# First weights in pieces beside the inputs, part of the banded attention's elementwise work on GpSimd, and one row maximum over two PSUM banks

## What is computed

```python
for l in range(2):                                   # kind A
    proj = rms_norm(x, norm_mix_w[l]) @ w_in[l]
    mixed = concat(blocked_gqa(q, k, v), ssd_mixer(...))
    x = x + mixed @ w_out[l]
    h = rms_norm(x, norm_ffn_w[l])
    x = x + (silu(h @ w_gate[l]) * (h @ w_up[l])) @ w_down[l]
x = rms_norm(x, final_norm_w)                        # "residual scaling"
for l in range(2):                                   # kind B
    proj = rmsnorm(x, g_attn[l]) @ w_in_2[l]
    ya = windowed_gqa_sink(qa, ka, va, sink[l])      # keys within 128 tokens
    yb = diff_attention(qb, kb, vb, lam)             # softmax 1 - lam * softmax 2
    x = x + concat(ya, norm(yb)) @ w_out_2[l]
    x = x + (silu(conv3(h @ gate)) * (h @ val)) @ w_down_2[l]
```

## Time and profile before

| | |
|---|---|
| time of the kernel before | 2509.87 us median of 3 runs (2509.07 to 2510.38) |
| profiled execution: time, and span from first to last instruction | 2512.78 us, 2510.6 us |
| busy share: PE, DVE, ACT, POOL | 97%, 59%, 38%, 8% |
| granted TensorE clock, mean | 0.991 of full speed |
| first matmul starts | 13.55 us |
| banded attentions, window of each | layer 2: 1366 to 1434 us; layer 3: 1993 to 2062 us |

### The profile page before, as it was taken

The page is one execution under the profiler, slowest core; times in us unless marked ns, Lnnn a source line. Parts: engine busy times, 40 slices in busy tenths (PEclk is TensorE's granted clock), DMA queues, the critical chain, the costliest instruction groups (busy, mean ns, idle before and its releaser), DMA issues.

```text
span 2510.6 us, 30919 instructions
## 1 busy us (share of the span) xinstructions
PE 2430.3 (97%) x12468; PEld 1989.0 (79%) x12468; DVE 1474.9 (59%) x2074; ACT 944.8 (38%) x1496; POOL 210.5 (8%) x143
## 2 busy tenths in 40 slices
PE   7999999999999999999999799999999989999999
PEld 6767888888876788888887578888888767888887
DVE  5867543435586754343567766545466776655554
ACT  4465322213446432222444563222243465322222
POOL 2001200000200110000132011000012101100000
PEclk9999999999999999999999899999999999999999
DMA  4200222222311032222321002222232110222222
GB/s 172 78 35 1 101 96 89 101 101 101 102 68 35 1 103 99 101 95 90 118 84 68 35 9 102 94 100 101 91 111 99 53 35 25 94 101 101 100 85 101
DMA packets 30238, 205.32 MB, mean 82 GB/s; under 512 B 3344, under 2 KB 3472, under 8 KB 6288
## 3 DMA queue, kind: packets, MB, share of 16 engines
q1 hardware_dynamic: 30096, 203.35, 22.8%
HBM read 201.24 MB, written 2.10 MB: 81 GB/s over the span
## 4 chain that ended last, share of the span: by engine, by line
PE 85%; DVE 8%; DVEq 3%; ACT 2%; issue 1%; ACTq 0%; DMA 0%; POOL 0%; SPq 0%
PE bank L1568 25%; PE bank L1570 25%; PE bank L1569 25%; PE bank L1727 1%; PE bank L1671 1%; PE bank L1703 1%; PE bank L1953 1%; PE bank L1901 1%; PE bank L1714 1%; PE bank L1654 1%; DVE w_lo L771 1%; DVE b_p L1435 1%; DVE neg_max L1423 1%; ACT w_hi L321 1%; DVEq L1430 1%
## 5 line engine op out<-in xcount | busy, mean ns | idle before, releaser
L771 DVE TENSOR_TENSOR w_lo<-w_raw,w_hi 128x2048 fp32r<-128x2048 f32 (+1 forms) x190 | 434.0, 2284 | 404.9 <-ACT w_hi L321 404.4
L1568 PE MATMUL bank<-h_ffn_hi,w_hi 128*128 128x512 f32 x1408 | 548.6, 390 | 0.0
L1570 PE MATMUL bank<-h_ffn_hi,w_lo 128*128 128x512 f32 x1408 | 547.8, 389 | 0.0
L1569 PE MATMUL bank<-h_ffn_lo,w_hi 128*128 128x512 f32 x1408 | 547.7, 389 | 0.0
L321 ACT ACTIVATE w_hi<-w_raw 128x2048 fp32r<-128x2048 f32 (+1 forms) x190 | 360.1, 1895 | 473.0 <-PE bank L1570 424.5
L1570 PEld LDWEIGHTS bank<-h_ffn_hi,w_lo 128*128 128x128 f32 x1408 | 264.3, 188 | 55.1
L1569 PEld LDWEIGHTS bank<-h_ffn_lo,w_hi 128*128 128x128 f32 x1408 | 264.3, 188 | 54.7
L1568 PEld LDWEIGHTS bank<-h_ffn_hi,w_hi 128*128 128x128 f32 x1408 | 264.3, 188 | 54.5
L1568 PE MATMUL bank<-act_hi,w_hi 128*128 128x512 f32 x704 | 273.9, 389 | 0.0
L1569 PE MATMUL bank<-act_lo,w_hi 128*128 128x512 f32 x704 | 273.9, 389 | 0.0
L1570 PE MATMUL bank<-act_hi,w_lo 128*128 128x512 f32 x704 | 273.9, 389 | 0.0
(11 more groups left out here) (305 smaller groups left out, 3396.3 us busy)
## 6 DMA issues: line engine op xcount, KB each, us to landing
w_raw<-weights SPq DMA_DIRECT2D x186, 1024.0 KB, 4.7
w_raw<-weights SPq DMA_DIRECT2D x4, 544.0 KB, 3.7
residual<-x_in SPq DMA_DIRECT2D x8, 256.0 KB, 5.8
x_out<-residual SPq DMA_DIRECT2D x8, 256.0 KB, 2.0
cst<-consts SPq DMA_DIRECT2D x1, 960.0 KB, 10.2
par_b<-params_b SPq DMA_DIRECT2D x1, 627.0 KB, 11.2
par_a<-params_a SPq DMA_DIRECT2D x1, 244.0 KB, 2.7
```

The costliest lines, as they stand in the source:

```text
L771: nc.vector.tensor_tensor(w_lo[s][:, cols], w_raw[s][:, cols], w_hi[s][:, cols].bitcast(F32), ALU.subtract).then_inc(w_ready, 1)
L1568: mm(out, ahi, bhi, start=start, stop=False)
L1569: mm(out, ahi, blo, start=False, stop=False)
L1570: return mm(out, alo, bhi, start=False, stop=stop)
```

## The change

- **Start.** Weights 0 and 1 come as 8 quarters of 128 x 512, each ahead of one tile of x. ACT, DVE split a quarter and then a tile of x, with the square of a tile one tile later. `first_pair` on PE goes over the 8 feature tiles, each with all four token tiles, and has `stats(0)` ahead of the last feature tile.
- **Opening of kind B.** ACT splits group `g0 + 2` before it waits for `rstd`.
- **Banded attention.** ACT splits groups `g0 + 9` and `g0 + 10` in halves, in steps 4, 5 and 8, 9. GpSimd makes their remainders, one instruction of 128 x 2048 each. In layer 2 GpSimd also scales `residual`, with two instructions of 128 x 4096, one behind each remainder. DVE waits for both before the additions of the output projection.
- **Row maxima.** In all three attentions one DVE instruction reduces both banks of a step. The 8 banks become one tensor for it.

```diff
@@ -181,11 +181,18 @@
...
         gate, silu, up = ([Fb[f"{n}{j}"] for j in range(2)] for n in ("gate", "silu", "up"))
-        bank = [ctx.enter_context(nc.psum_tensor(f"bank{j}", [P, 512], F32)) for j in range(8)]
+        banks = ctx.enter_context(nc.psum_tensor("bank", [P, 8, 512], F32))
+        bank = [banks[:, j, :] for j in range(8)]
+
+        def both_banks(pair, width):
+
+            return banks[:, pair[0]:pair[1] + 1, 0:width]
         par_in = sem("par_in")
+        first_in = [sem(f"first_in{k}") for k in range(KT)]
+        first_hi, first_ready = sem("first_hi"), sem("first_ready")
         x_arrived = [sem(f"x_arrived{k}") for k in range(KT)]
...
@@ -293,10 +304,10 @@
             sp.dma_start(par_a[:, :, :], params_a).then_inc(par_in, 16)
-            sp.dma_start(w_raw[0][:, :], weights[0]).then_inc(w_in[0], 16)
             for k in range(KT):
+                cols = first_cols(k)
+                sp.dma_start(w_raw[k // 4][:, cols], weights[k // 4][:, cols]).then_inc(first_in[k], 16)
                 sp.dma_start(residual[:, k, :], x_in[:, k, :]).then_inc(x_arrived[k], 16)
-            sp.dma_start(w_raw[1][:, :], weights[1]).then_inc(w_in[1], 16)
             sp.dma_start(cst[:, :], consts).then_inc(consts_in, 16)
...
@@ -314,11 +325,20 @@
...
                 s = g % 2
-                act.wait_ge(w_in[s], 16 * (g // 2 + 1))
-                if g >= 2:
-                    act.wait_ge(bank_done, 2 * (g - 2) + 2)
+                act.wait_ge(w_in[s], 16 * (g // 2))
+                act.wait_ge(bank_done, 2 * (g - 2) + 2)
                 cols = slice(0, width_of(g))
                 nc.scalar.activation(w_hi[s][:, cols], w_raw[s][:, cols], ACT.Copy).then_inc(w_hi_done, 1)
+
+            def split_half(g, part):
+
+                s = g % 2
+                act.wait_ge(w_in[s], 16 * (g // 2))
+                act.wait_ge(bank_done, 2 * (g - 2) + 2)
+                cols = slice(part * GW // 2, (part + 1) * GW // 2)
+                nc.scalar.activation(w_hi[s][:, cols], w_raw[s][:, cols], ACT.Copy)
+                if part == 1:
+                    act.drain().then_inc(w_hi_done, 1)
             def wait_tile(lay, tile):
@@ -467,12 +487,15 @@
...
             act.wait_ge(par_in, 16)
-            split_hi(0)
             for k in range(KT):
+                cols = first_cols(k)
+                act.wait_ge(first_in[k], 16)
+                nc.scalar.activation(w_hi[k // 4][:, cols], w_raw[k // 4][:, cols], ACT.Copy).then_inc(w_hi_done if k % 4 == 3 else first_hi, 1)
                 wait_tile(-1, 24 + k)
                 norm_hi(h_mix_hi, k, mix_weight(0, k))
-                norm_square(0, k)
-            split_hi(1)
+                if k >= 1:
+                    norm_square(0, k - 1)
+            norm_square(0, KT - 1)
             for lay in range(LAYERS):
...
@@ -675,8 +698,8 @@
...
                 nc.scalar.activation(lam[:, 2:4], lam[:, 0:2], ACT.Exp).then_inc(lam_out, 1)
+                split_hi(g0 + 2)
                 act.wait_ge(rstd_ready, 2 * lay + 1)
-                split_hi(g0 + 2)
                 for half in range(2):
...
@@ -706,8 +729,8 @@
...
                         sink_exp(i // 4 - 1)
-                    if i in (12, 14):
-                        split_hi(g0 + 3 + i // 2)
+                    if i in (4, 5, 8, 9):
+                        split_half(g0 + IN_B + i // 8, i % 2)
                     if i - 1 in TURN_STEPS:
...
@@ -891,11 +914,9 @@
             def pair_max(lay, i):
-                for par_ in range(2):
-                    c = 2 * i + par_
-                    dve.wait_ge(s_done, 32 * lay + c + 1)
-                    nc.vector.tensor_reduce(neg_max[:, c:c + 1], bank[S_BANKS[i % 2][par_]][:, :], AX.X, ALU.max,
-                                            negate=True).then_inc(max_done, 1)
+                dve.wait_ge(s_done, 32 * lay + 2 * i + 2)
+                nc.vector.tensor_reduce(neg_max[:, 2 * i:2 * i + 2], both_banks(S_BANKS[i % 2], 512), AX.X, ALU.max,
+                                        negate=True).then_inc(max_done, 2)
             def pair_copy(lay, u, width, pts):
@@ -968,10 +989,15 @@
...
             dve.wait_ge(par_in, 16)
-            split_lo(0)
             for k in range(KT):
+                s, cols = k // 4, first_cols(k)
+                if k % 4 == 3:
+                    dve.wait_ge(w_hi_done, s + 1)
+                else:
+                    dve.wait_ge(first_hi, 3 * s + k % 4 + 1)
+                nc.vector.tensor_tensor(w_lo[s][:, cols], w_raw[s][:, cols], w_hi[s][:, cols].bitcast(F32),
+                                        ALU.subtract).then_inc(w_ready if k % 4 == 3 else first_ready, 1)
                 norm_lo(0, h_mix_hi, h_mix_lo, k, mix_weight(0, k))
-            split_lo(1)
             dve.wait_ge(consts_in, 16)
...
@@ -1367,11 +1393,9 @@
                 def window_max(i):
-                    for par_ in range(2):
-                        c = 2 * i + par_
-                        dve.wait_ge(s_done, base + c + 1)
-                        nc.vector.tensor_reduce(neg_max[:, c:c + 1], bank[S_BANKS[i % 2][par_]][:, 0:window(i // 4)[1] * P],
-                                                AX.X, ALU.max, negate=True)
+                    dve.wait_ge(s_done, base + 2 * i + 2)
+                    nc.vector.tensor_reduce(neg_max[:, 2 * i:2 * i + 2], both_banks(S_BANKS[i % 2], window(i // 4)[1] * P),
+                                            AX.X, ALU.max, negate=True)
                     dve.drain()
...
@@ -1404,12 +1428,6 @@
...
                         pair_copy(lay, i - 2, window((i - 2) // 4)[1] * P, pts)
-                    if i in (12, 14):
-                        split_lo(g0 + 3 + i // 2)
-                    if l == 0 and 7 <= i < 7 + KT:
-                        k = i - 7
-                        nc.vector.scalar_tensor_tensor(residual[:, k, :], residual[:, k, :], par_a[:, 0, A_FIN + k:A_FIN + k + 1],
-                                                       rstd_bc[:, :], ALU.mult, ALU.mult)
                     if i >= 6 and i % 4 == 2:
...
@@ -1476,6 +1492,9 @@
...
                     nc.vector.memset(gate[j][:, SEQ + 1:SEQ + 2], 0.0)
+                if l == 0:
+                    dve.wait_ge(x_scaled, 1)
+                dve.wait_ge(w_ready, g0 + IN_B + 2)
                 for g in range(QUARTERS):
...
@@ -1548,6 +1567,25 @@
...
                                                 ALU.pow).then_inc(hrs_ready, 1)
+
+                def split_lo(g):
+
+                    s = g % 2
+                    pool.wait_ge(w_ready, g)
+                    pool.wait_ge(w_hi_done, g + 1)
+                    nc.gpsimd.tensor_tensor(w_lo[s][:, :], w_raw[s][:, :], w_hi[s][:, :].bitcast(F32), ALU.subtract).then_inc(w_ready, 1)
+
+                g0 = FIRST[lay]
+                split_lo(g0 + IN_B)
+                if l == 0:
+                    pool.wait_ge(bc_ready, broadcasts(2 * lay) + 1)
+                    x = residual[:, :, :]
+                    nc.gpsimd.tensor_tensor(x, x, par_a[:, 0, A_FIN:A_FIN + KT].unsqueeze(2).to_broadcast([P, KT, SEQ]), ALU.mult)
+                    pool.drain()
+                    split_lo(g0 + IN_B + 1)
+                    nc.gpsimd.tensor_tensor(x, x, rstd_bc[:, :].unsqueeze(1).to_broadcast([P, KT, SEQ]), ALU.mult).then_inc(x_scaled, 1)
+                else:
+                    split_lo(g0 + IN_B + 1)
                 def diff_factors(t):
...
@@ -1605,6 +1643,25 @@
...
                 last.then_inc(bank_done, 1)
+
+            def first_pair():
+
+                for k in range(KT):
+                    s, kk = divmod(k, 4)
+                    if kk == 3:
+                        pe.wait_ge(w_ready, s + 1)
+                    else:
+                        pe.wait_ge(first_ready, 3 * s + kk + 1)
+                    pe.wait_ge(h_ready, k + 1)
+                    if k == KT - 1:
+                        pe.wait_ge(consts_ready, 1)
+                        stats(0)
+                    for t in range(TB):
+                        ts_, ws = slice(t * P, (t + 1) * P), slice(kk * 2 * COLS, (kk + 1) * 2 * COLS)
+                        last = three(bank[pair_bank(0, t)][:, :], h_mix_hi[:, k, ts_], h_mix_lo[:, k, ts_], w_hi[s][:, ws], w_lo[s][:, ws],
+                                     k == 0, k == KT - 1)
+                        if kk == 3 and t % 2 == 1:
+                            last.then_inc(bank_done, 1)
             def token_pair(g):
@@ -1802,15 +1859,16 @@
...
                 g0 = FIRST[lay]
-                enter(g0)
-                for half in range(2):
-                    pair_half(g0, 0, half, 2 * lay)
-                enter(g0 + 1)
-                pair_half(g0, 1, 0, 2 * lay)
                 if lay == 0:
-                    pe.wait_ge(consts_ready, 1)
-                stats(2 * lay)
-                pair_half(g0, 1, 1)
+                    first_pair()
+                else:
+                    enter(g0)
+                    for half in range(2):
```

(10 more changed lines are left out.)

9 lines of the change are left out of this document (2 added, 7 removed).

## The result

The changed kernel takes **2524.93 us** (median of 5 runs, 2521.26 to 2525.61) against 2510.08 (2509.07 to 2512.81, 5 runs): ratio **1.0054, 95% interval 1.0043 to 1.0066**. The change makes the kernel slower by 0.54%, some 14 us. The forecast of 2510 was wrong, and its range, to 2521, too short. The profiled execution took 2524.93, of which 2523.1 is span: 12.5 more than in the profile before. (The profiled run of the kernel before, 2512.78, lies 2.7 above the median; by the medians the difference is 14.9.)

A forecast was written before the change was run, and what follows sets the result against it. TensorE, busy for 97% of the span, was taken as the bound, with gains only where it waits. The terms, -5.9 - 3.6 + 11.0 - 1.0 - 0.5 = 0.0, gave 2510 us, range 2487 to 2521.

The forecast's parts named there:

- Term 1: Start: quarters of weights 0 let the first matmul and the statistics begin earlier, -5.9 us (bounds -3.5 and -7.5).
- Term 2: Opening of layers 2 and 3: ScalarE's chain moves up by 1.91 us and TensorE's waits go, -3.6 us.
- Term 3: Layer 2's banded attention: VectorE's waits behind GpSimd and the clock outweigh the gain from moved splits, +11.0 us.
- Both races: Layer 2's two remainders: GpSimd or VectorE's line 1377 first was open; one loss taken, 2.7 us more each time.
- Term 4: Layer 3's banded attention: gain of 5.7 us from moved splits, less waits behind GpSimd's remainders, -1.0 us.
- Term 5: Row maxima: -1.5 us in banded and differential attention, +1.0 in full attention from later exponentials, -0.5 us together.
- Port shared: Rival: VectorE and GpSimd share the port without holding it, so GpSimd's work is free; -24.2 us, 2486, chance 0.15.
- GpSimd first at all four: Rival: GpSimd comes first at each banded-attention remainder and runs at its dear bounds; +10.4 us, 2520, chance 0.25.
- Start short: Rival: quarters and tiles feed TensorE slower than 2.7 us a tile; start gives about -2 us, 2514, chance 0.10.

The follow-up runs named there:

- start_only: The kernel before with the new start alone (weights 0 and 1 in quarters, splits tile by tile, squares one tile later): 2503.2 us.
- m_all_apart: The 2484.7 us kernel (change with scaling on VectorE, remainder after rstd, full-attention maxima apart, column-wise sink minimum) with all maxima bank by bank: ratio 0.9903, against 0.9898.
- one_input: The changed kernel with VectorE's sink minimum, sink sum and denominator addition in the banded attention done column by column, one SBUF input each: 2511.0 us.
- m_min_pair: The 2484.7 us kernel (change with scaling on VectorE, remainder after rstd, full-attention maxima apart, column-wise sink minimum) with that minimum two-input again: 17.2 us slower by medians.

## Why the prediction was wrong

**Term 1, the start: right.** -6.25 by the trace, -5.65 by the medians of `start_only`, -5.9 forecast. The parts were less exact than the sum: the first matmul came at 7.84, not 7.2, but the slow matmuls behind it were fewer (9 in 3.95 us; I had 14 in 6, and the trace before has 11 in 6.0), so the statistics started at 28.81 (29.1 forecast). From there to group 2 it took 4.8 us, as forecast.

**Term 2, the openings: the step that failed.** Forecast -3.6, measured +2.1. "ScalarE's chain moves up by its 1.91 us, and both waits go" counted the moved instruction and not what it sets free: VectorE's remainder, which had waited for it, now starts right behind `var`, and holds the port against the power that `rstd` needs. I had stated this very lock two paragraphs on, and applied it in the banded attention alone. The first evictions, which were to come 1.9 us earlier behind the statistics, came 0.25 and 0.15 us later; with the power first they come 1.8 earlier. That restores the step, and the openings then gain 0.7 to 3.1 us (2.2 on average over five traces), still less than the forecast. For there was a second slip: the 2.8 us of layer 3 in the earlier trace rows belong to the group behind the rope, not to `g0 + 2`; that wait never went, in any kernel here.

**Term 3, layer 2's banded attention: right in mechanism and nearly in size.** +10.4 with the joint maxima against +11.0. The gain was 8.3 instead of 7.5, GpSimd's sizes 4.51, 7.01 and 8.84 (4.5, 8.9 and 8.9 taken). Both races went to GpSimd, where I had one of two (+2.7). These three misses, -0.8, -1.9 and +2.7, cancel, so that the sum fits is in part luck. The first race was lost for this: ScalarE's half of `w_hi` starts right behind the exponentials of step 4, at 1384.17, and GpSimd was 0.20 us ahead, while the fused maximum brought the minimum no earlier.

**Term 4, layer 3: mis-sized.** Forecast -1.0, measured +2.9. The gain was there (8.2 us for steps 12 to 15 where it was 14.68), but both remainders came first, the minima lasting 4.33 and 4.38 us where I had 1.0 twice and 2.7 once, and the clock behind them was not counted: the stage loses 9.4 against its gain of 6.5, 1.0 more than the waits of 8.4. Against `start_only`, whose stage is 1.76 shorter than in the trace before, the miss would be larger.

**Term 5, the maxima: mis-sized.** The full attentions: +1.0 forecast, 3.7 by the ledger and 4.0 by thirteen traces, near the upper bound of 4.7, and 3.3 of it stand in TensorE's waits. TensorE's busy share of 92% in the earlier trace rows says that little is idle, and not that a later exponential is hidden. The gain of 1.5 elsewhere was not seen (`m_all_apart`: 2.5 by the medians, not clear of noise).

The misses are -0.35 (start), +5.7, -0.6, +3.9, +2.7 and +1.2 (the rest): 12.5 us, the whole difference of the spans; by the scatter of such stages, each is sure to 1 or 2 us only.

**The rivals.** *Port shared* is out: `one_input` and `m_min_pair` each change only the second SBUF input and move the waits away or back. *GpSimd first at all four* came true, as half of the rival, at the sizes that I had taken or less and not the dear ones; alone it would have given 2515. *Start short* is out. In the Trainium skill, SBUF — State Buffer, section "SBUF: two separate sides", the sentence on whichever engine starts first covers both directions; the trace agrees (3.00 us for a power of 128 x 4, 7.39 for a minimum of 128 x 2). The prediction used the lock for VectorE behind GpSimd; it held the other way round too.

## What to carry to other kernels

When an edit lets an instruction start earlier, follow what stood behind it: here a freed remainder took a port that a 1 us instruction on the critical chain needed, and one added wait gave some 5 us. Before work goes to GpSimd, list VectorE's instructions with two SBUF inputs in its shadow, the smallest first: on the path each can cost nearly the whole GpSimd instruction and the clock behind it, and the one-input form of a single minimum, in four steps of two layers, was worth 17 us here. Where two engines race for a port within 0.2 us, price the loser's case. A joint reduction saved VectorE some 0.06 us a step and delayed the first consumer by 0.5; it can pay only where nobody waits for the first half, and no run here showed it paying.

## What the runs showed of the hardware

- The wait for the port does not depend on how little the waiting instruction has to do: up to 7.39 us for 128 x 2, which takes 0.16 alone. GpSimd's 128 x 2048 takes 4.5 us, 128 x 4096 7.0 with one value per tile as second operand and 8.8 with a second operand of full rows.
- VectorE's `tensor_scalar` on one column of SBUF with a per-partition operand does not wait for GpSimd (0.34 us for two, beside instructions of 4.5 and 7.0).
- The lock works against GpSimd as well: a power of 128 x 4 took 3.00 instead of 1.02 us.
- Behind TensorE's idle time in the first three waits of `m_min_pair` (3.57, 2.99 and 3.57 us) the granted clock was 0.50, 0.66 and 0.66 over 5 us; behind the fourth (0.58 us) it was 1.00. In layer 2 the stage lost 10.8 us against waits of 8.0.
- The same full attention, with the same 4.6 us of waits, took 52.5 us at a granted clock of 1.00 and 54.1 at 0.97.
- Layer 3's banded attention, with the same code, was 5.1 us shorter in one trace than in another (-2.2 and +2.9), with one race between the engines won in the one (by 0.13 us) and lost in the other (by 0.16).
